# Sorted experts in three turns of fp32 lanes, with a ring of 14 places

## The reference

```python
def swiglu(h, w1, w3, w2):
    return (jax.nn.silu(h @ w1) * (h @ w3)) @ w2

def moe_swiglu(h, router, w1, w3, w2):
    logits = (h @ router).astype(jnp.float32)
    top_vals, top_idx = lax.top_k(logits, TOP_K)
    top_w = jax.nn.softmax(top_vals, axis=-1)
    combine = jnp.sum(jax.nn.one_hot(top_idx, N_EXPERTS, dtype=jnp.float32) * top_w[..., None], axis=-2)
    y = jnp.zeros(h.shape, jnp.float32)
    for e in range(N_EXPERTS):
        y = y + combine[..., e:e + 1] * swiglu(h, w1[e], w3[e], w2[e]).astype(jnp.float32)
    return y.astype(h.dtype)
```

## Time and profile before

| | before |
|---|---|
| median of 3 runs | 1438.59 us (1438.42 to 1442.12) |
| the profiled execution | 1438.85 us |
| its span | 1437.1 us, granted clock 0.993 |
| PE, PEld, DVE, ACT busy | 90%, 63%, 54%, 41% of the span |
| moved | 426.5 MB, 297 GB/s over the span |

### The profile page before, as it was taken

One profiled execution on the slowest core, in us unless ns is written; L12 is line 12 of the kernel. 1 busy time (PEld: TensorE's weight loads), 2 busy tenths in 40 slices (PEclk: granted clock), 3 DMA queues, 4 the chain that ended last, 5 costly groups with the idle time before them and its releaser, 6 DMA issues.

```text
span 1437.1 us, 16492 instructions
## 1 busy us (share of the span) xinstructions
PE 1297.9 (90%) x6600; PEld 904.1 (63%) x6600; DVE 781.2 (54%) x907; ACT 594.3 (41%) x666; POOL 60.7 (4%) x73
## 2 busy tenths in 40 slices
PE   6999999999999899997766889999999777678998
PEld 6864999998874678832222368888884222226886
DVE  5996544445997688810000078888882000006887
ACT  4274443334365577700000167776771000005774
POOL 1042000000042000000000000000000000000000
PEclk9999999999999999999999999999999999999999
DMA  7650755525640599999999999999998999999993
GB/s 250 234 176 1 264 184 196 177 71 167 229 153 1 211 354 367 366 332 397 396 393 393 399 390 395 380 359 355 352 360 302 394 396 395 393 398 391 393 389 116
DMA packets 203847, 426.51 MB, mean 297 GB/s; under 512 B 7410, under 2 KB 48626, under 8 KB 203764
## 3 DMA queue, kind: packets, MB, share of 16 engines
q1 hardware_dynamic: 202448, 424.90, 81.1%
q10 hardware_dynamic: 1316, 0.49, 0.1%
HBM read 424.31 MB, written 1.05 MB: 296 GB/s over the span
## 4 chain that ended last, share of the span: by engine, by line
PE 65%; DMA 21%; DVE 11%; issue 1%; ACT 1%; SPq 0%; ACTq 0%; POOL 0%; DVEq 0%
DMA ring<-in_moe_w 20%; PE bank L2124 7%; PE bank L2125 7%; PE bank L2126 7%; PE bank L2201 7%; DVE arena L1113 6%; PE bank L2137 4%; PE bank L2138 4%; PE bank L2139 4%; PE bank L2007 3%; PE bank L2006 3%; PE bank L2005 3%; PE bank L1834 2%; PE bank L1635 2%; PE bank L2214 2%
## 5 line engine op out<-in xcount | busy, mean ns | idle before, releaser
L1084 DVE TENSOR_TENSOR w_split<-ring,w_split 128x2048 fp32r<-128x2048 f32 x201 | 460.0, 2291 | 183.5 <-ACT w_split L679 183.3
L679 ACT CAST w_split<-ring 128x2048 fp32r<-128x2048 f32 x201 | 383.8, 1911 | 208.3 <-PE bank L2126 90.0
L2201 PE MATMUL bank<-ring,hT 128*64 128x512 f32 x896 | 206.7, 605 | 68.8 <-DMA ring<-in_moe_w 68.7
L1536 DVE TENSOR_TENSOR hn<-hn,bank 128x512 f32<-128x512 f32 x42 | 28.7, 683 | 372.1 <-PE bank L2201 372.1
L2201 PEld LDWEIGHTS bank<-ring,hT 128*64 128x64 f32 x896 | 70.3, 138 | 193.8 <-issue 193.8
L2124 PE MATMUL bank<-w_split,xe_hi 128*128 128x512 f32 x448 | 181.2, 405 | 6.6 <-DVE w_split L1084 6.6
L2125 PE MATMUL bank<-w_split,xe_hi 128*128 128x512 f32 x448 | 178.1, 398 | 0.0
L2126 PE MATMUL bank<-w_split,xe_lo 128*128 128x512 f32 x448 | 177.9, 397 | 0.0
L938 ACT ACTIVATE hn<-bank 128x512 f32<-128x512 f32 x42 | 25.3, 601 | 352.4 <-PE bank L2201 352.4
L2214 PE MATMUL bank<-ring,hT 128*64 128x512 f32 x448 | 102.3, 597 | 35.8 <-DMA ring<-in_moe_w 35.8
L1113 DVE SCALAR_TENSOR_TENSOR arena<-arena,par 128x256 f32<-128x256 f32 x240 | 103.6, 500 | 0.1
(11 more groups left out here) (263 smaller groups left out, 1588.8 us busy)
## 6 DMA issues: line engine op xcount, KB each, us to landing
ring<-in_moe_w SPq DMA_DIRECT2D x336, 1024.0 KB, 11.2
ring<-in_dense_w SPq DMA_DIRECT2D x33, 1024.0 KB, 5.4
ring<-in_w_in SPq DMA_DIRECT2D x8, 1024.0 KB, 9.8
ring<-in_w_in SPq DMA_DIRECT2D x4, 2048.0 KB, 8.3
ring<-in_w_out SPq DMA_DIRECT2D x4, 2048.0 KB, 8.0
ring<-in_cmp_k_w SPq DMA_DIRECT2D x2, 2048.0 KB, 14.1
ring<-in_cmp_v_w SPq DMA_DIRECT2D x2, 2048.0 KB, 9.4
ring<-in_w_in SPq DMA_DIRECT2D x2, 1120.0 KB, 12.6
```

The source lines that it names most:

```text
L679: nc.scalar.copy(split_part(0, t), raw(t)).then_inc(w_hi_ready, 1)
L1084: V.tensor_tensor(split_part(1, t), raw(t), split_part(0, t).bitcast(F32), ALU.subtract).then_inc(w_lo_ready, 1)
L2201: mm = T.matmul(bank[b][half_slots(a), :], xs[:, kk, half_slots(a)], w[a][:, k, :], start=(kk == 0), stop=(kk == KD - 1))
```

## The change

The expert stage is written anew.

- The experts, still sorted by count with expert 0 first, are worked off in three turns of 3, 3 and 2 experts (`RANKS`). A turn has one or two *lanes*: 128 slots each, that is one pass over the array's 128 columns. A lane is cut into tiles, each given as (expert of the turn, first slot of that expert, number of slots, first column). `SHARED` (turn 0) has two lanes of three tiles, 32, 32 and 64 columns wide: expert 0 has 96 slots in the first, the third largest 96 in the second, and the next 64 slots, half in each. `MIXED` (turn 1) has one lane for the largest expert, 128 wide, and one with two tiles of 64. `PAIRED` (turn 2) has one lane with two tiles of 64.
- All expert matmuls are float32, with no split: `high_part` and `low_part` remain only in the dense part.
- The ring has 14 places (`RING`): eight in `ring`, six in `scratch`, where `w_split` stands in the dense part and attention keeps probabilities. `places` works out beforehand which piece goes to which place and after which use. Twelve pieces of expert 0 (e1 and e3 of three chunks) are fetched before the order is known; after that its e1 and e3 pieces stay up to six ahead of their use (`LEAD`).
- A piece of an expert that sits in both lanes is used twice, and its place is free after the second. `order_ready` now comes right after `perm`.
- Chunks alternate between the lanes: e1 of both, then e3 and the e2 of the chunk before. The scatter of a turn sums over its lanes in PSUM. The loop for overflow goes once over all eight experts.

```diff
+    RING = 14
+    FIRST_PARTS = (4, 5, 6, 7, 8, 9, 10, 11, 12, 13, 0, 1, 2, 3)
+    HALF, QUARTER = P // 2, P // 4
+    SHARED = (((2, 0, QUARTER, 0), (0, HALF, QUARTER, QUARTER), (0, 0, HALF, HALF)),
+              ((2, QUARTER, QUARTER, 0), (1, HALF, QUARTER, QUARTER), (1, 0, HALF, HALF)))
+    MIXED = (((0, 0, P, 0),), ((1, 0, HALF, 0), (2, 0, HALF, HALF)))
+    PAIRED = (((0, 0, HALF, 0), (1, 0, HALF, HALF)),)
+    WHOLE = (((0, 0, P, 0),), ((0, P, P, 0),))
+    RANKS = ((0, 2, 3), (1, 4, 5), (6, 7))
+    LANES = (SHARED, MIXED, PAIRED)
+    LEAD = 6
...
+            for t in range(TURNS):
+                w = {}
+                for m, (kind, c, half, who) in enumerate(FETCH[t], PARTS[0][t]):
+                    s, _, after = PLACE[m]
+                    if after is not None:
+                        sp.wait_ge(w_used, BASE + after)
+                    elif s in tenant:
+                        sp.wait_ge(*last_read(tenant[s]))
+                    else:
+                        sp.wait_ge(o_psum, NT * L)
...
+                    fetch(w[who], s, kind, c, half)
...
+            def up(j, lanes, kind, c, n):
+
+                number = (2 * c + (kind == "e3")) * len(lanes) + n
+                b = UP_BANK[number % 3]
...
+                for half in range(2):
+                    if number == 0:
+                        pe.wait_ge(xs_ready, nth(j, FOUR, 3 + half))
+                    w = arrived(j, lanes, n, kind, c, half)
+                    for k in range(4):
+                        kk = 4 * half + k
+                        for t, tile in enumerate(lanes[n]):
+                            mm = T.matmul(bank[b][rows_of(tile), :], xs[:, kk, slots_of(n, tile)], w[tile[0]][:, k, :],
+                                          start=(kk == 0), stop=(kk == KD - 1))
+                            if k == 3 and t in last_tiles(lanes[n]):
+                                mm.then_inc(w_used, 1)
...
+                for c in range(FCH):
+                    for n in range(len(lanes)):
+                        up(j, lanes, "e1", c, n)
+                        if c >= 1:
+                            transposes(j, lanes, c - 1, n)
+                    if c == 0 and previous is not None:
+                        scatter(j - 1, previous, BACK_BANK)
+                    for n in range(len(lanes)):
+                        up(j, lanes, "e3", c, n)
...
+                        if c >= 1:
+                            down(j, lanes, c - 1, n)
```

More of the change, by code:

```diff
@@ L107, in hymba_trunk @@
[L107 to L112, removed]
+    assert E == 8 and BASE % SPLIT == 0
+    RING = 14
+    FIRST_PARTS = (4, 5, 6, 7, 8, 9, 10, 11, 12, 13, 0, 1, 2, 3)
@@ new lines, in fetches @@
+    def fetches(lanes, lead):
+        order = list(dict.fromkeys(key[:4] for key in uses(lanes)))
+        if lead == 0:
+            return order
+        own = [key for key in order if key[3] == 0 and key[0] != "e2"]
+        got, ahead, met = own[:2 * lead], own[2 * lead:], 0
+        for key in order:
+            if key not in own:
+                got.append(key)
+            else:
+                met += 1
+                if met > lead and ahead:
+                    got.append(ahead.pop(0))
+        return got + ahead
@@ L114, in hymba_trunk @@
+    PLACE, FILLED = places()
     ctx = ExitStack()
@@ L395, in selected @@
[L395 to L411, removed]
@@ L1611, in _ @@
+            for t in range(TURNS):
+                turn(t, LANES[t], t + 1 if t + 1 < TURNS else None)
+            add_back(TURNS - 1, LAST_BACK_BANK)
+            more = dv.value_load(trips_i[0:1, 0:1], min_val=0, max_val=1)
+            with dv.If(more > 0):
+                with dv.Fori(0, E) as j:
+                    select_again(j)
+                    turn(j, WHOLE)
+                    add_back(j, BACK_BANK)
         @block.tensor
@@ L2209, in down @@
+            def down(j, lanes, c, n):
+                pe.wait_ge(actT_ready, nth(j, STEPS, step(lanes, c, n) + 1))
+                if c == 0 and n == 0 and not (isinstance(j, int) and j == 0):
+                    pe.wait_ge(added, nth(j, FOUR, 0))
+                for half in range(2):
+                    w = arrived(j, lanes, n, "e2", c, half)
                     for k in range(2):
@@ new lines, in own_slots @@
+            def own_slots(j, lanes, n, columns):
+                pe.wait_ge(actT_ready, nth(j, STEPS, step(lanes, 1, len(lanes) - 1) + 1 + n * len(lanes)))
+                for i in range(NT):
+                    T.transpose(bank[T_BANK][:, i * P:(i + 1) * P], sel[:, i, n * P:(n + 1) * P], ident[:])
+                for i in range(NT):
+                    for tile in lanes[n]:
+                        last = T.matmul(bank[T_BANK][rows_of(tile), S:S + 1], sel[:, i, slots_of(n, tile)],
+                                        wgt_tab[:, i, bass.ds(columns[tile[0]], 1)], start=(i == 0), stop=(i == NT - 1))
+                last.then_inc(own_psum, 1)
@@ L2271, in _ @@
-                pe.wait_ge(xe_ready, (TURNS + PASS + 1) * (2 * QB))
-            scatter((more, 0))
+                with pe.Fori(0, E) as j:
+                    pe.wait_ge(sel_ready, nth(j, SELECTS, SELECTS[1]))
+                    for q in range(4):
+                        if q == 3:
+                            pe.wait_ge(xs_ready, nth(j, FOUR, 1))
+                        gather(WHOLE, q)
+                    turn(j, WHOLE, (j + E,))
+                    scatter(j, WHOLE, BACK_BANK)
 def kernel(**inputs):
```

790 lines of the change are left out of this document (299 added, 491 removed).

## The result

| | before | after |
|---|---|---|
| median | 1438.53 us (1438.42 to 1442.12, 4 runs) | **1734.77 us** (1733.48 to 1738.36, 4 runs) |
| ratio | | 1.2056, interval 1.2030 to 1.2082 |
| span of the profiled execution | 1437.1 us | 1736.6 us |
| PE, PEld, DVE, ACT busy | 90, 63, 54, 41% | 95, 40, 21, 15% |

The kernel takes 20.6% more time. The likeliest case (1375 us) did not come true; the rival "widths in turn" (1745 us, given 0.33) did.

A forecast was written before the change was run, and what follows sets the result against it. PE and DMA were taken to bind by stage, then DMA after a near-balanced turn 0: 486.5 + 2.1 + 324 x 2.66 = 1350, about 10 us idle, last landing 1361, 3.4 and 8.5 us more, span 1373, time 1375 us; range 1357 to 1745.

The forecast's parts named there:

- The likeliest case: Turn 0's three tiles run side by side at 0.858 us a step: 1375 us, own range 1357 to 1400, chance 0.52.
- widths in turn: Array empties between 32- and 64-column tiles: 2.02 us a step, turn 0 takes 701 us, kernel 1745 us; chance 0.33.
- the unknown: Turn 0's step of tiles 32, 32 and 64 columns wide: between 0.858 and 2.02 us, taken as 0.858.
- the 0.15 us: Cost of a change of tile shape on PE, read from L1791's entry from L1785 and exit to L1774.
- Single file: At most two records at a time: turn 0's step 1.29 us, kernel 1499 us; 0.13 with anything between (1400 to 1520).
- The early fetch doesn't help: Before the stage: twelve pieces no earlier than now, five pieces or 13 us lost, 1388 us; within the 0.52 case.
- the stall for want of places: Expert stage's start: only two of 14 places open beside the twelve early pieces, so DMA idles about 10 us.
- DMA's rate: Expert weights move at 394 GB/s, 2.66 us a piece; the skill's 358 GB/s would mean an end near 1464.
- The sum, given its own premise: Whole kernel at 0.858 us a step: last landing 1361, then the end, span 1373, time 1375 us.
- 3.4 + 8.5: After the last landing: 3.4 us for four steps of the last half of e2, about 8.5 for the end.
- The split of the gain: Span against before: 47 us by the last landing, 12 at the end, the rest by the start.
- The point of decision: Turn 0's step above 1.1 us outlasts the time gained; end at 1066 + 336 x step, 1375 where that is less.

The follow-up runs named there:

- e2: Not a follow-up run here: a part of each expert's matmul work, in two blocks by two banks a half, done for the chunk before; no measured time of its own.

## Why the prediction was wrong

**The step that failed** is the value taken for the unknown, the step of tiles of 32, 32 and 64 columns. The prediction bounded it by 0.858 us (three chains side by side) and 2.02 (nothing overlaps between widths, and each change costs), and took 0.858 as "nearest to the rows of two tiles". It is 1.985. Each half of the array does run its own sequence, but only while the widths are equal. The argument was that the 0.15 us stands "only where the next instruction also wants columns that were just in use". The rows didn't show this: every change of shape in the earlier trace rows was on shared columns, so they could not tell shared columns from changed shape. The late first load of the earlier trace rows was the better hint: the prediction named it for the rival and yet gave the rival 0.33.

**The rival's price was right.** 4 x 0.429 + 2 x 0.15 = 2.02 us a step, against 1.985; a change costs 0.136 us (widths grouped) where 0.15 was read from two rows. Turn 0 was to take 701 us from 495.5 to 1196; in the profile it takes 688, from 502 to about 1190. The total was to be 1745 and is 1735. The Trainium skill, "TensorEngine Tiling (Array Packing)", section Key Properties, says that changing the tiling mode drains the engine; the mixed tiles in either kernel agree with it, and equal tiles, which change nothing, run at 0.86.

**Single file** is refuted: four records start together in the run with four narrow tiles. **"The early fetch doesn't help"** supposed that only seven or so of the twelve pieces would be down in time. The profiles show all twelve down: the six of the scratch are issued from 458.9 us on, and nothing is left to move from 484 to 492 (0 GB/s). Its price, 13 us for five pieces, did not hold: with eight early pieces instead of twelve the kernel is 5 us faster. Only having none costs time, 17 us. The prediction had the stall for want of places in its sum, but not that fewer early pieces would avoid it.

**DMA's rate** held where DMA sets the pace: slices of 392 to 397 GB/s after turn 0, and 394 and 389 in turns 1 and 2 of the run with four narrow tiles. In its turn 0, with the stall at the start, DMA carried 378. The Trainium skill's figure of about 358 GB/s ("DMA: Bandwidth & Descriptors", section Specifications) would have put the end near 1464 us by the prediction's estimate; the kernels with tiles of one width and early pieces are at 1381 to 1389, so these runs don't bear it out.

**The sum, given its own premise**, was 1375 us; the run with four narrow tiles, which fulfils the premise, takes 1386.6. Its chain of waits ends so:

```profile
1352.29 18.67 DMA scratch<-in_moe_w
1370.96 0.14 issue
1371.10 3.67 PE bank L2069 x16
1374.80 0.69 ACT ye L989
1375.49 0.04 issue
1375.53 3.71 PE bank L2096 x8
1379.27 0.69 DVE x_sb L1088
```

The last piece lands at 1370.96, not 1361: 811 us at 391 instead of 394 GB/s are 6 us of this, the rest lies at the start. From there to the end 13.0 us pass, against 3.4 + 8.5 predicted. The split of the gain (47 us by the last landing, 12 at the end) was off in itself: by the earlier trace rows the last piece before landed at 1410 us or later, 49 us after 1361, and the end then gives 15. The stall of "about 10 us" at the start, for want of open places, is there with 11. The stage was to start at about 495.5 us and starts at 496.45. The six scratch pieces were to be issued at 458 us and to land between 460 and 478; in the profile after they are issued from 458.9 on and have landed by 477.5, and DMA moves 376 GB/s from 460 to 480. Turn 2 was to show PE idle for some 60 us: in the run with four narrow tiles it is 221 - 164 = 57.

**The point of decision.** The formula 1066 + 336 x step held at both steps that were measured: 1733 us for 1.985 (1734.77 measured) and 1664 for 1.78 (1666.13). The 1.1 us beside it is where the formula reaches the time before, 1436 us. PE overtakes DMA sooner, at 0.92 us, where it passes 1375; no run has a step between 0.86 and 1.78.

## What to carry to other kernels

Give all tiles that the array works on at a time the same width, and cut a wide tile into narrow ones rather than mix: eight records of 32 columns took 0.86 us where six of two widths took 1.98. When an unknown is bounded by two rows, ask which of the differences between them and the new case they vary; rows that never separate two causes give no weight to either. And a place filled early is a place not open for what is needed next: of 14, filling eight or ten was some 5 us better than filling twelve.

## What the runs showed of the hardware

- A change of the stationary tile's width separates the matmuls before from those after it, also on other columns of the array (at least 0.522 us between the starts at each of 671 changes, where equal tiles start together), and costs 0.136 us beyond that. Loads are not made ahead across it.
- Four fp32 tiles of 32 columns run side by side, four records every 0.43 us, at the rate of one full-width matmul, the tile at columns 96 to 127 among them. 1792 narrow records took the busy time of 896 of twice their width (207.7 and 206.7 us).
- Tiles pair by their order in the instruction stream: with the order 32, 64, 32 the pair forms across two steps.
- The granted clock may stand at the half level from 476 us in one execution (0.54 from 476 to 484) and only from 484 on in another of the same kernel (1.00 from 476 to 484), and be back some 4 us later too; the stage then started 5.5 us later.
